# Up-projection of a gated MLP: a pair of k tiles as seven products, its weight sums built in DRAM

## The reference

```
def conv_ffn(x, norm2_g, w_up, conv_w, conv_b, w_down):
    h = rms_norm(x, norm2_g)
    u = h @ w_up                      # (256, 2048) @ (2048, 11008)
    u = causal_depthwise_conv(u, width 3) + conv_b
    gate, val = jnp.split(u, 2, axis=-1)
    return x + (jax.nn.silu(gate) * val) @ w_down
```

## Time and profile before

| | us |
|---|---|
| median of 3 runs | 1039.6 (1039.22 to 1039.84) |
| profiled execution, its time | 1040.04 |
| profiled execution, its span | 1038.3 |
| TensorE busy | 1032.1 |
| VectorE busy | 802.0 |
| ScalarE busy | 800.5 |

### The profile page before, as it was taken

How to read it: one execution, slowest core, us unless ns; L and a number is a source line. 1 busy time by engine, 2 the same in 40 slices (tenths; PEclk the granted TensorE clock), 3 DMA queues, 4 the chain that set the end, 5 groups by cost and what they waited for, 6 DMA issues and landing times.

```text
span 1038.3 us, 16511 instructions
## 1 busy us (share of the span) xinstructions
PE 1032.1 (99%) x5275; PEld 934.2 (90%) x5275; DVE 802.0 (77%) x1354; ACT 800.5 (77%) x1406; POOL 21.6 (2%) x27
## 2 busy tenths in 40 slices
PE   9999999999999999999999999999999999999998
PEld 8999999999988888888888888888889988888887
DVE  6888888878766665586776876867768699989998
ACT  6776676888857885879788788797887789856663
POOL 0201011000000000000000000000000000000000
DMA  9666777777765655665565565655655656556654
GB/s 357 232 186 214 219 242 213 229 245 233 250 231 196 202 201 203 203 208 202 190 220 193 199 215 193 214 196 196 217 180 195 230 175 241 204 196 226 205 205 162
DMA packets 81437, 221.04 MB, mean 213 GB/s; under 512 B 20312, under 2 KB 24544, under 8 KB 81248
## 3 DMA queue, kind: packets, MB, share of 16 engines
q1 hardware_dynamic: 81232, 220.07, 62.9%
q10 hardware_dynamic: 144, 0.20, 0.1%
HBM read 214.32 MB, written 5.91 MB: 212 GB/s over the span
## 4 chain that ended last, share of the span: by engine, by line
PE 82%; DVE 10%; DMA 4%; ACT 2%; issue 1%; SPq 0%; DVEq 0%; ACTq 0%
PE ps L711 14%; PE ps L710 14%; PE ps L712 14%; PE ps L501 5%; PE ps L502 5%; PE ps L503 5%; PE ps L739 4%; PE ps L741 4%; PE ps L740 4%; DVE w_lo L1312 3%; PE ps L691 3%; PE ps L690 3%; PE ps L689 3%; DMA raw<-in_wrest 1%; DMA raw<-in_win 1%; DVE sums_lo_t L1881 1%
## 5 line engine op out<-in xcount | busy, mean ns | idle before, releaser
L1312 DVE TENSOR_TENSOR w_lo<-raw,w_hi 128x1024 fp32r<-128x1024 f32 (+2 forms) x406 | 457.2, 1131 | 185.6 <-ACT w_hi L836 184.2
L836 ACT ACTIVATE w_hi<-raw 128x1024 fp32r<-128x1024 f32 (+2 forms) x406 | 393.4, 977 | 145.6 <-PE ps L712 53.1
L710 PE MATMUL ps<-w_hi,xs 128*128 128x512 f32 (+1 forms) x704 | 263.4, 374 | 0.0
L711 PE MATMUL ps<-w_lo,xs 128*128 128x512 f32 (+1 forms) x704 | 263.4, 374 | 0.0
L712 PE MATMUL ps<-w_hi,xs 128*128 128x512 f32 (+1 forms) x704 | 263.4, 374 | 0.0
L501 PE MATMUL ps<-w_hi,xs 128*128 128x384 f32 (+1 forms) x496 | 165.0, 333 | 0.6 <-DVE w_lo L1312 0.5
L502 PE MATMUL ps<-w_lo,xs 128*128 128x384 f32 (+1 forms) x496 | 161.8, 326 | 0.0
L503 PE MATMUL ps<-w_hi,xs 128*128 128x384 f32 (+1 forms) x496 | 161.8, 326 | 0.0
L712 PEld LDWEIGHTS ps<-w_hi,xs 128*128 128x128 f32 x704 | 133.1, 189 | 17.2
L711 PEld LDWEIGHTS ps<-w_lo,xs 128*128 128x128 f32 x704 | 133.1, 189 | 17.2
L710 PEld LDWEIGHTS ps<-w_hi,xs 128*128 128x128 f32 x704 | 133.1, 189 | 17.2
(11 more groups left out here) (229 smaller groups left out, 1143.3 us busy)
## 6 DMA issues: line engine op xcount, KB each, us to landing
raw<-in_wrest SPq DMA_DIRECT2D x278, 512.0 KB, 3.8
raw<-in_win SPq DMA_DIRECT2D x117, 384.0 KB, 3.7
raw<-in_wrest SPq DMA_DIRECT2D x16, 384.0 KB, 3.0
p_scratch<-pdT SPq DMA_DIRECT2D x14, 192.0 KB, 2.8
p_read<-p_scratch SPq DMA_DIRECT2D x56, 48.0 KB, 2.7
xtok<-in_xtok SPq DMA_DIRECT2D x4, 512.0 KB, 14.0
xv<-in_xtok SPq DMA_DIRECT2D x4, 512.0 KB, 5.6
raw_ahead<-in_w SPq DMA_DIRECT2D x5, 392.0 KB, 7.7
```

Source lines behind the costliest of these rows:

```text
L710: pe.matmul(o, xh, wh, start=(k == 0), stop=False, skip_group_check=True)
L711: pe.matmul(o, xh, wl, start=False, stop=False, skip_group_check=True)
L836: act.activation(slot(w_hi, s, w), slot(raw, s, w), ACT.Copy).then_inc(hi_ready, 1)
L1312: dve.tensor_tensor(slot(w_lo, s, w), slot(raw, s, w), f32(slot(w_hi, s, w)), ALU.subtract).then_inc(split_done, 1)
```

## The change

In batches 1 to 8, the k tiles 6 and 7 are no longer two pieces of 12 matmuls each. Seen as blocks, h is tokens (0, 1) by k (6, 7) and the weights are k (6, 7) by (gate, value); their product is made with seven block products (21 matmuls) in place of eight (24).

- The two pieces become four: "left" (the gate half of k tile 6, 512 columns), "lower" (all of k tile 7), "two" and "more" (sums of weight blocks, 1024 columns each). A batch has 18 pieces in the rings, and the ring of four slots stays. "lower" and "more" are positions at which ScalarE and VectorE only split; the jobs of steps 6 and 7 stand at "left" and "two".
- GpSimd builds the weight sums in DRAM (`t_scratch`), six DMAs per batch, each waiting for the one before; three of them add to what stands at their destination. The build of batch q + 1 starts when piece OUT0 + 8 + 16 q is used. SP waits for it (`t_built`) ahead of "two".
- The sums of blocks of h are made once, in batch 0, by VectorE (five operations) and split into high and low parts.
- Four of the products go, alone, into the banks of the other parity, which have to be evacuated first (TensorE waits for `u_evac` at k = 6). At k = 8 and 9 ScalarE copies the first of them and VectorE forms four sums with 512-column operations; ScalarE scales these at steps 12 and 15; the next batch's TensorE waits for them.
- For the batches with sums VectorE, not ScalarE, takes the four banks out, each with a scalar_tensor_tensor of 512 columns that adds the scaled sums: two of them in step 0, two in step 1 behind the first transpose.
- The semaphores of two norms are shared. Down-projection and the other stages stay as they are.

The core of the diff (the helper functions for counts, widths and h's sums, and changed numbers of pieces, are left out):

```diff
+UP_SEVEN, UP_BATCHES = (6,), (1, 8)
+UP_SUMS = len(UP_SEVEN) * (UP_BATCHES[1] - UP_BATCHES[0] + 1)
+UP_LONG, UP_EXTRA = KT + 2 * len(UP_SEVEN), 2 * UP_SUMS
+OUT_PIECES, UP_PIECES, DOWN_PIECES = KT * KT // 8, (FULL + 1) * KT + UP_EXTRA, FT * KT // 8
...
+UP_ADD, UP_SCALE = (8, 9), (12, 15)
...
+        def up_first(nb):
+            if not isinstance(nb, int):
+                return nb * UP_LONG + (UP0 + KT - UP_LONG)
+            return UP0 + KT * nb + (UP_LONG - KT) * min(max(nb - UP_BATCHES[0], 0), UP_BATCHES[1])
+        def up_parts(nb):
+            if not with_sums(nb):
+                return [("piece", k) for k in range(KT)]
+            parts = []
+            for k in range(KT):
+                if k in UP_SEVEN:
+                    parts += [(kind, k) for kind in ("left", "lower", "two", "more")]
+                elif k - 1 not in UP_SEVEN:
+                    parts.append(("piece", k))
+            return parts
+        def up_job(part):
+            kind, k = part
+            return {"piece": k, "left": k, "two": k + 1}.get(kind)
...
+            def up_pieces(nb, par):
+                n = len(UP_SEVEN)
+                for j, (kind, k) in enumerate(up_parts(nb)):
+                    s = up_at(nb, par, j) % RING
+                    sp.wait_ge(split_done, up_first(nb) + (j - RING + 1))
+                    if kind in ("two", "more"):
+                        q = (nb - UP_BATCHES[0]) * n + UP_SEVEN.index(k)
+                        c = 0 if kind == "two" else PW
+                        if kind == "two":
+                            sp.wait_ge(t_built, 96 * (q + 1))
+                        sp.dma_start(slot(raw, s), t_d[q * P:(q + 1) * P, c:c + PW]).then_inc(raw_landed[s], 16)
+                        continue
+                    w = BLOCK if kind == "left" else PW
+                    row = (UP0 - IN_PIECES + nb * KT + k + (kind == "lower")) * P
+                    sp.dma_start(slot(raw, s, w), wrest_d[row:row + P, 0:w]).then_inc(raw_landed[s], 16)
+            rest_pieces(OUT0 + 8, UP0 + KT, PW, 0)
+            for nb in range(UP_BATCHES[0], UP_BATCHES[1] + 1):
+                up_pieces(nb, nb % 2)
...
+            def up_seven(nb, par, k, j):
+                n = UP_SEVEN.index(k)
+                first, last = n == 0, n == len(UP_SEVEN) - 1
+                own, shared = UP_BANKS[par], UP_BANKS[1 - par]
+                def a(kk, m):
+                    return [xs[:, (k + kk) * 2 * S + m * S + h * P:(k + kk) * 2 * S + m * S + (h + 1) * P] for h in range(2)]
+                def a_sum(i):
+                    return [h_sum(n, i, h) for h in range(2)]
+                def b(jj, half):
+                    at = up_at(nb, par, j + jj) % RING
+                    return [weave(slot(t, at, BLOCK, half * BLOCK)) for t in (w_hi, w_lo)]
+                def product(to, x, w, start=False, stop=False):
+                    pe.matmul(bank(to), x[0], w[0], start=start, stop=False, skip_group_check=True)
+                    pe.matmul(bank(to), x[0], w[1], start=False, stop=False, skip_group_check=True)
+                    return pe.matmul(bank(to), x[1], w[0], start=False, stop=stop, skip_group_check=True)
+                if first:
+                    pe.wait_ge(u_evac, nb * 4)
+                if isinstance(nb, int) and nb == UP_BATCHES[0]:
+                    pe.wait_ge(h_lo, n + 1)
+                pe.wait_ge(split_done, up_first(nb) + (j + 1))
+                product(shared[0], a(0, 0), b(0, 0), first, last).then_inc(piece_used, 1)
+                pe.wait_ge(split_done, up_first(nb) + (j + 2))
+                product(own[0], a(1, 0), b(1, 0))
+                product(own[1], a_sum(3), b(1, 1)).then_inc(piece_used, 1)
+                pe.wait_ge(split_done, up_first(nb) + (j + 3))
+                product(shared[2], a_sum(1), b(2, 0), first, last)
+                product(shared[3], a_sum(0), b(2, 1), first, last).then_inc(piece_used, 1)
+                pe.wait_ge(split_done, up_first(nb) + (j + 4))
+                end = product(shared[1], a_sum(2), b(3, 0), first, last)
+                if last:
+                    end.then_inc(c_ended, 1)
+                product(own[2], a(1, 1), b(3, 1)).then_inc(piece_used, 1)
...
+                if not isinstance(nb, int) or UP_BATCHES[0] < nb <= UP_BATCHES[1] + 1:
+                    pe.wait_ge(c_summed, nb * 4 - 4)
+                for j, (kind, k) in enumerate(up_parts(nb)):
                     if isinstance(nb, int) and nb == 0:
                         pe.wait_ge(h2_ready, k + 1)
-                    up_piece(nb, k, UP_BANKS[par], w)
+                    if kind == "piece":
+                        up_piece(nb, par, k, j, w)
+                    if kind == "left":
+                        up_seven(nb, par, k, j)
...
             def up_steps(pb, s, par, tiles=BATCH):
                 if s < 2:
-                    evacuate_up(pb, s, par, tiles * P)
+                    if not with_sums(pb):
+                        evacuate_up(pb, s, par, tiles * P)
                 elif s < 10:
...
+            def take_first(nb, par):
+                act.wait_ge(c_ended, nb)
+                act.wait_ge(u_evac, nb * 4)
+                act.activation(c_tile(0, 0), bank(UP_BANKS[1 - par][0]), ACT.Copy).then_inc(c_first, 1)
+            def scale_sums(nb, m):
+                act.wait_ge(c_summed, nb * 4)
+                act.activation((x1sq, x1f)[m][:], (x1sq, x1f)[m][:], ACT.Copy, scale=r2[:, m:m + 1]).then_inc(c_scaled, 1)
+            def up_batch(nb, par, post=True, spill=True, ahead=UW, last=False, turn=None):
+                for j, part_ in enumerate(up_parts(nb)):
+                    s = up_job(part_)
+                    split_hi(up_first(nb) + (j + 4), up_at(nb, par, j + 4) % RING, up_round(nb, par, j + 4, turn),
+                             up_width(nb, j + 4, ahead))
+                    if s is None:
+                        continue
+                    if with_sums(nb):
+                        if s == UP_ADD[0]:
+                            take_first(nb, par)
+                        if s in UP_SCALE:
+                            scale_sums(nb, UP_SCALE.index(s))
+                    if not post and 10 <= s < 10 + len(UP_SEVEN):
+                        h_sums_hi(s - 10)
...
+                if s == 0 and with_sums(pb):
+                    evacuate_sums(pb, 0, par)
                 if s in (1, 2):
                     turn_up(pb, s - 1, tiles * P)
+                if s == 1 and with_sums(pb):
+                    evacuate_sums(pb, 1, par)
...
+            def up_sums(nb, par, step):
+                m6, m5, m7 = [bank(UP_BANKS[1 - par][i]) for i in (1, 2, 3)]
+                if step == 0:
+                    dve.wait_ge(c_first, nb)
+                    dve.wait_ge(u_evac, nb * 4)
+                    dve.tensor_tensor(c_tile(1, 1), m6, c_tile(0, 0), ALU.subtract).then_inc(c_summed, 1)
+                    dve.wait_ge(c_summed, nb * 4 - 3)
+                    dve.tensor_tensor(c_tile(0, 1), m5, c_tile(1, 1), ALU.add).then_inc(c_summed, 1)
+                if step == 1:
+                    dve.tensor_tensor(c_tile(1, 0), m7, c_tile(1, 1), ALU.subtract).then_inc(c_summed, 1)
+                    dve.wait_ge(c_summed, nb * 4 - 1)
+                    dve.tensor_tensor(c_tile(1, 1), c_tile(0, 1), m7, ALU.subtract).then_inc(c_summed, 1)
+            def evacuate_sums(pb, m, par):
+                dve.wait_ge(piece_used, up_first(pb) + UP_LONG)
+                dve.wait_ge(c_scaled, pb * 2 + (m - 1))
+                dve.wait_ge(u_turned, pb * 2)
+                for gv in range(2):
+                    at = (2 * m + gv) * UW
+                    dve.scalar_tensor_tensor(out=ut[:, at:at + UW], in0=bank(UP_BANKS[par][2 * m + gv]), scalar=r2[:, m:m + 1],
+                                             in1=c_tile(m, gv), op0=ALU.mult, op1=ALU.add).then_inc(u_evac, 1)
             def up_batch(nb, par, post=True, spill=True, ahead=UW, last=False):
-                for s in range(KT):
+                for j, part_ in enumerate(up_parts(nb)):
+                    s = up_job(part_)
                     if not post and s == 1:
                         x1_add(OUT_BLOCKS - 1)
-                    split_lo(nb * KT + (UP0 + s + 4), s % RING, 2 * (ahead if s >= 12 else LW if last else UW))
+                    split_lo(up_first(nb) + (j + 4), up_at(nb, par, j + 4) % RING, up_width(nb, j + 4, ahead))
+                    if s is None:
+                        continue
+                    if with_sums(nb) and s in UP_ADD:
+                        up_sums(nb, par, UP_ADD.index(s))
+                    if not post and 9 <= s < 9 + len(UP_SEVEN):
+                        h_sums(s - 9)
+                    if not post and 11 <= s < 11 + len(UP_SEVEN):
+                        h_sums_lo(s - 11)
...
+            def build_sums(q):
+                nb, n = q // len(UP_SEVEN) + UP_BATCHES[0], q % len(UP_SEVEN)
```

(92 more changed lines are left out.)

34 lines of the change are left out of this document (16 added, 18 removed).

## The result

The changed kernel takes 1075.8 us (median of 4 runs, 1074.82 to 1075.92) against 1039.7 us (1039.22 to 1039.94) of the kernel before, run beside it. The ratio is 1.0346, 95% interval 1.0334 to 1.0359: 36 us slower. The prediction was 1068, range 1056 to 1083.

The account below looks back on a forecast made before the run. TensorE, busy for 99% of the span, was taken to bound the kernel. Batches 2 to 8 (+25.2), batch 1 (+1.25) and loads (+2) summed to +28.5 us: 1068.5 profiled, about 1068 in the median, range 1056 to 1083.

Parts of the forecast that it names:

- The likeliest case: Whole kernel: TensorE waits at the short pieces, +28.5 us in sum, about 1068 us in the median; chance 63%.
- rival 2: Loads crowded out by POOL's queue beside the builds: 1071, or 1081 and up to 1090 us; chance 12%.
- Products: Up-projection: 21 matmuls instead of 24 per pair of pieces, saving 0.65 us per batch, 5.2 us in eight batches.
- Evacuation: VectorE's four added operations at a batch's start: 0.66 us each, making ScalarE's first move 1.37 us late.
- The walk: VectorE, ScalarE and TensorE followed in time through a batch: +3.60 us per batch for batches 2 to 8, +25.2.
- reload of weights: TensorE loading weights before its first product after a wait: 0.21 us, once per batch.
- Batch 1: Up-projection's batch 1, with batch 0 still evacuated by ScalarE and the transposes earlier: +1.25 us.
- Building: Weight sums built in DRAM by six DMAs in turn per batch: some 25 to 30 us each, not late.
- rival 3: Late builds: a build takes 60 us and SP stands at "two"; about +79, 1119 us or a little less; chance 5%.
- Loads beside the builds: Piece loads beside batches 1 to 5: landings of 4.8 us, 0.4 us each, +2 us in all.
- Rival 1: Half of it: VectorE's evacuations do not delay the second transpose; +1.7 us per batch, +13, 1053 us; chance 12%.
- Rival 4: Faster: ScalarE stays ahead and TensorE never waits in the up-projection; 1034.4 us; chance 6%.

Follow-up runs that it names:

- e1: Changed kernel without the builds in DRAM: plain pieces of w_up loaded as "two" and "more", weight sums left out; 1064.9 us.
- e2: Kernel of e1 with ScalarE taking the four banks out as before the change, scaled sums formed but not added; 1049.7 us.
- e6: Kernel of e1 with ScalarE's sixteen moves spread 2, 1, 1, 1, 2, 3, 3, 3 over steps 2 to 9; 1064.6 us (one run).
- e7: Changed kernel with the three accumulating DMAs of each build as plain copies of the same bytes; 1070.1 us.
- e3: Kernel before the change with the same eight builds in DRAM added, their result read by nobody; 1039.3 us, ratio 1.0000.
- e4: Changed kernel, whole, with the builds moved ahead, two in flight, from input piece 72 on; 1104.1 us.
- e8: Changed kernel without builds or weight sums, VectorE's order as in e5, ScalarE's moves spread 3, 2, 1, 1, 2, 2, 2, 3; 1045.8 us.
- e5: Changed kernel, whole, with VectorE doing the four evacuations and both transposes ahead of the low parts at a batch's start; 1067.0 us.

## Why the prediction was right, and where a term was off

The direction and the range hold. The likeliest case holds for all but the builds (e1: 25.5 us against 26.5 forecast), and its mechanism is shown and not only argued: e2 gives back the evacuation's part (15.2 us). The builds' part came by rival 2's mechanism, and it is what lies between 1068 and 1075.8. The range was also less than the prediction's own bounds add up to: +13 and +8 on 1068 give 1089, not 1083.

- *Products*: 0.65 us per batch, measured 0.64 (e6).
- *Evacuation*: 0.66 us each and 1.37 us of delay; measured 0.66 and 13.04 - 11.61 = 1.43.
- *The walk*: +3.60 per batch, measured 3.59 in batch 7 (batch 8 has the same waits to 0.01). Its reload of weights was wrong in its parts: 0.21 us once per batch. In the rows at 706.73, 709.42 and 711.82 the first product begins with its weight load, not 0.21 behind it, and the next starts 0.31 to 0.33 later instead of 0.22. So the cost was about 0.1. Two terms that were too small made up for it: the moves begin 0.06 later than forecast (13.04, 12.98), and a product starts 2.36 to 2.37 after the high part of its piece, not 2.32. That the sum is right to 0.01 is luck; that it is right to 0.1 us is not.
- *Batch 1*: +1.25, measured 42.35 - 41.43 = +0.92 (0.95 in e1): right in kind, 0.3 too high.
- *e1 as a whole*: 25.2 + 1.25 = 26.5 was forecast for all but the builds; measured 25.5, by the medians.
- *Building*: a build of 25 to 30 us was forecast. The first took from 309.2 to 347.6, and the eight took 35.7 to 39.0. The accumulating DMA of 512 KB lands after 8.9 us, the plain copy of the same size after 5.0; of these 3.9 us 2.8 are the accumulation, since the same transfer made plain takes 6.1 (e7). No load waited for a build: the limit was 50 us. So rival 3 stays out.
- *Loads beside the builds*: this is the term that was mis-sized. The prediction had landings of 4.8 us, the measured median, and made +2 us of it. It cost 10.9 (1075.8 - 1064.9); the waits at "lower" give 10.2, the 0.8 above among them. The step that failed is "0.4 us each": it took the median for every load, but a late load of 8 us costs by its own length, once there is no margin, and the margin was spent by the same change. That is rival 2's mechanism, at 12%, and at about twice the +5 of its first price. The rule of the Trainium skill that was named there (DMA: Bandwidth & Descriptors, "Queues, rings and completion order"), that a DMA engine serves its queues in turn, agrees with e3 and e4, in so far as beside a second busy queue single loads of the first take nearly twice the time (8.6 and 11.3 us against 4.6 and 6.7 at most); no row shows single packets taking turns.
- *Rival 1* (half of it) fails in the change. e2, where VectorE has no evacuations, comes near it: 1.34 us per batch against 1.7, 1049.7 against 1053. *Rival 4* fails: even e8 does not reach 1034.

## What to carry to other kernels

Saving products makes a piece shorter for TensorE, but not for the engines that prepare it: read how far ahead each piece is ready, in order of time, at the very place where the pieces get shorter, and compare that with what the other engines' queues hold there. A mean of 7 or 11 us of slack per batch said nothing here, since ScalarE stood idle for 2.6 us and then had none. And transfers that cost nothing beside the old kernel must be priced against the margin that the new one leaves.

## What was not expected of the hardware

The clock. After the 3.16 us in which TensorE waited for "lower" in the longest batch, its rows and the granted clock of the following stretches are:

```profile
567.97 0.79 PE L815 MATMUL ps<-w_hi,xs 128*128 128x512 f32 x1 [3.16 <-DVE w_lo L1468]
568.56 0.63 PE L816 MATMUL ps<-w_lo,xs 128*128 128x512 f32 x1
```
```profile
568.00:570.00 2.00, 2.00 (x5) 1.64 (x6) 1.41 (x3) 1.95 (x3) 0.56 (x1) 0.50 0.59 173
570.00:572.00 2.00, 2.00 (x8) 1.34 (x7) 1.17 (x3) 1.93 (x4) 0.00 (x0) 0.65 0.69 250
```

From 568 to 570 us the clock is at 0.50, its lower level of 1.2 GHz, and a matmul starts every 0.43 us instead of 0.22. Before, TensorE never waited so long in this part, and after the waits of 0.4 to 1.2 us in batches 7 and 8 the clock stays at 1.00.

It cost next to nothing here. The first product of "two" starts 2.72 us after that of "lower"; in batch 7, at the full clock, it is 2.70, since TensorE would only have waited longer for "two". So in this execution the builds' cost is the wait and not the clock. The four executions of the changed kernel had mean granted clocks of 0.998, 0.997, 0.994 and 0.989, and their times differ by 1.1 us. Where TensorE waits for nothing behind the fall, it costs in full: 3.1 us in e5, where it came in whole pieces.

Nor does the length of the wait alone decide. Two matmul starts 3.54 us apart were followed by the lower level (567.97) and two 3.34 apart were not (661.70); in other runs 2.85 us were (e7, 471.73) and 3.35 were not (e5, 517.49). What decides is not shown.
